# Loads of x moved into the weights' DMA queue, samples' products in another buffer, second norm's scale and shift on two engines

## The reference

```python
h = rms_norm(x, g) * (1 + sc1) + sh1
x = x + g1 * mixer(h)
h = rms_norm(x, g) * (1 + sc2) + sh2
x = x + g2 * (relu(h @ w1) ** 2 @ w2)     # 1024 -> 4096 -> 1024
```

## Time and profile before

| | us |
|---|---|
| median of 3 runs | 1322.38 (1321.24 to 1323.36) |
| profiled execution, its own time | 1323.73 |
| its span on the slowest core (core 3) | 1322.2 |
| spans of the 8 cores | 1315.9 to 1322.2 |
| TensorE busy on core 3 | 1255.1 (95%) |
| VectorE, ScalarE, GpSimd busy | 765.4, 587.5, 45.2 |

### The profile page before, as it was taken

The page is one execution under the profiler, slowest core; times in us unless marked ns, Lnnn a source line. Parts: engine busy times, 40 slices in busy tenths (PEclk is TensorE's granted clock), DMA queues, the critical chain, the costliest instruction groups (busy, mean ns, idle before and its releaser), DMA issues.

```text
span 1322.2 us, 21660 instructions; the slowest of 8 cores (1315.9 to 1322.2 us)
## 1 busy us (share of the span) xinstructions
PE 1255.1 (95%) x7558; PEld 670.3 (51%) x7558; DVE 765.4 (58%) x1478; ACT 587.5 (44%) x1088; POOL 45.2 (3%) x87
## 2 busy tenths in 40 slices
PE   3299999999999999999999999999999999999995
PEld 0156565555555555555444444554545555554543
DVE  4287856545445454577657657854545445454567
ACT  5349443433333333466443555533333333333474
POOL 0001000000000000000000000000000000000000
PEclk9999999999999999999999999999999999999998
DMA  9999936434243342502000016511303031100024
GB/s 256 193 151 171 152 53 118 92 63 96 52 78 65 64 80 49 96 1 45 20 1 1 1 32 120 105 33 32 59 7 64 1 64 29 36 1 0 1 108 164
DMA packets 23880, 91.08 MB, mean 69 GB/s; under 512 B 2768, under 2 KB 10192, under 8 KB 15696
## 3 DMA queue, kind: packets, MB, share of 16 engines
q0 software_dynamic: 9392, 67.34, 28.7%
q1 hardware_dynamic: 14384, 22.35, 5.6%
HBM read 145.43 MB, written 11.01 MB: 118 GB/s over the span
## 4 chain that ended last, share of the span: by engine, by line
PE 89%; DMA 5%; ACT 2%; DVE 2%; issue 1%; POOL 0%; SPq 0%; DVEq 0%; ACTq 0%; POOLq 0%
PE ps L977 35%; PE ps L951 34%; PE ps L1126 5%; PE ps L1097 4%; PE ps L1213 4%; PE ps L793 2%; DMA ring<-w_pack 2%; PE ps L621 2%; DMA xT_sb<-x_pack 2%; ACT hT_sb L653 1%; PE ps L583 1%; PE ps L1128 1%; DVE xT_sb L1253 1%; DMA arena<-ln_b 1%; PE ps L1179 1%
## 5 line engine op out<-in xcount | busy, mean ns | idle before, releaser
L690 DVE SCALAR_TENSOR_TENSOR xT_sb<-ps,modT,xT_sb 128x512 f32<-128x512 f32 (+3 forms) x728 | 459.0, 638 | 440.5 <-PE ps L977 393.5
L977 PE MATMUL ps<-arena,ring 128*128 128x384 bf16 (+3 forms) x2624 | 521.7, 343 | 0.1
L951 PE MATMUL ps<-hT_sb,ring 128*128 128x384 bf16 (+2 forms) x2592 | 519.7, 345 | 0.0
L957 ACT ACTIVATE arena<-ps 128x384 bf16<-128x384 f32 (+3 forms) x324 | 169.6, 527 | 497.4 <-PE ps L951 497.3
L977 PEld LDWEIGHTS ps<-arena,ring 128*128 128x128 bf16 x2624 | 253.9, 98 | 215.6 <-issue 0.6
L951 PEld LDWEIGHTS ps<-hT_sb,ring 128*128 128x128 bf16 x2592 | 251.2, 98 | 216.2
L959 ACT ACTIVATE arena<-arena 128x384 bf16<-128x384 bf16 (+3 forms) x324 | 180.6, 561 | 28.8 <-ACT arena L957 2.2
L618 ACT ACTIVATE sq<-xT_sb 128x384 bf16<-128x384 f32 (+3 forms) x216 | 105.8, 530 | 72.1 <-DVE xT_sb L690 42.1
L643 DVE TENSOR_TENSOR hT_sb<-xT_sb,rstd 128x768 bf16<-128x768 f32 (+2 forms) x80 | 75.4, 1005 | 38.9 <-ACT rstd L635 38.8
L621 PE MATMUL ps<-sq,ones 128*128 128x384 bf16 (+3 forms) x216 | 49.0, 355 | 23.0 <-ACT sq L618 20.9
L1126 PE MATMUL ps<-ring,hT_sb 128*128 128x512 bf16 x272 | 67.2, 392 | 2.6 <-ACT arena L1102 2.6
(11 more groups left out here) (91 smaller groups left out, 467.6 us busy)
## 6 DMA issues: line engine op xcount, KB each, us to landing
ring<-w_pack POOLq DMA_DIRECT2D x62, 1024.0 KB, 9.0
xT_sb<-x_pack SPq DMA_DIRECT2D x3, 1536.0 KB, 21.6
xT_sb<-x_pack SPq DMA_DIRECT2D x2, 2048.0 KB, 18.9
y_pack<-xT_sb SPq DMA_DIRECT2D x8, 512.0 KB, 2.8
y_pack<-xT_sb SPq DMA_DIRECT2D x8, 384.0 KB, 2.5
ring<-w_pool POOLq DMA_DIRECT2D x1, 1024.0 KB, 24.1
y_pack<-xT_sb SPq DMA_DIRECT2D x4, 256.0 KB, 3.1
arena<-sp_pack POOLq DMA_DIRECT2D x1, 736.0 KB, 23.1
```

The costliest lines, as they stand in the source:

```text
L690: nodes.append(S.op("dve", lambda e: e.scalar_tensor_tensor(out=xs, in0=P_(v)[:, 0:n], scalar=mcol(l, vG, dco), in1=xs, op0=ALU.mult, op1= ...
L951: mms = [(lambda e, dc=dc: e.matmul(P_(v)[:, 0:n], pv(key, 512)[:, dc, fc * 128:(fc + 1) * 128], hT.ap()[:, dc, c0:c0 + n], start=(dc == 0 ...
L957: ev = S.op("act", lambda e: e.activation(out=av, in_=P_(v)[:, 0:n], func=AF.Relu), reads=[(v.key, 0, 1)], writes=ak, cost=c_act(n), vbs=[v])
L977: mms.append((lambda e, fc=fc, av=av: e.matmul(P_(v)[:, 0:w], pv(key, 1024)[:, fc, dco * 128:(dco + 1) * 128], av, start=(fc == 0), stop=( ...
```

## The change

DMA_RATE in the planner goes from 300 to 315 KB per us. The loads of x are issued from GpSimd's queue, each planned behind the piece before it: x of g0 and g1 first, x of g2 before ada 8, x of g3 and g4 before ada 10; `GATE` is gone. The order of the pieces is changed at block 1 (w1 block 1 comes before ada 0 and 1). The due times are set anew, and `pool_z` and `pool_P` of a group stand together. The second norm's `affine` is "mix" for every group: even channel chunks on ScalarE, odd ones on VectorE. `sample_pool` writes its residual products at HH, not at H3.

```diff
@@ -24,13 +24,14 @@
 
 ENGS = ("pe", "act", "dve", "pool", "sp")
 LAT = {"pe": 0.16, "act": 0.28, "dve": 0.24, "pool": 0.3, "sp": 0.3}
-DMA_RATE = 300.0e3
+DMA_RATE = 315.0e3
 DMA_LAT = 2.2
 TABLE_BIAS = 2.5
 
 PIECES = [("ada", 0, a) for a in (2, 3)] + [("wpool", 0, 0)] + [("ada", 0, a) for a in (4, 5, 8, 9, 6, 7)] \
-    + [("w1", 0, 0), ("ada", 0, 10), ("ada", 0, 11), ("w2", 0, 0), ("ada", 0, 0), ("ada", 0, 1)]
-for _b in range(1, 8):
+    + [("w1", 0, 0), ("ada", 0, 10), ("ada", 0, 11), ("w2", 0, 0), ("w1", 0, 1), ("ada", 0, 0), ("ada", 0, 1), ("w2", 0, 1),
+       ("ada", 1, 0), ("ada", 1, 1)]
+for _b in range(2, 8):
     PIECES += [("w1", 0, _b), ("w2", 0, _b)] + [("ada", 1, a) for a in range(2 * (_b - 1), min(12, 2 * _b))]
 PIECES += [(w, 1, h) for w in ("inu", "inv", "out") for h in range(2)]
 PIECES += [(w, 1, b) for b in range(8) for w in ("w1", "w2")]
@@ -517,14 +518,20 @@
     S.op("dve", lambda e: e.memset(hT.ap()[:, :, 0:16], 0.0), writes=HK(0, 16), cost=0.3)
     xoff = [8 * t0 for (t0, n) in GR]
 
-    def load_x(g, after=()):
+    prev = [None]
+
+    def queue(node):
+        prev[0] = node
+
+    def load_x(g):
         t0, n = GR[g]
-        S.op("sp", lambda e: e.dma_start(
+        queue(S.op("pool", lambda e: e.dma_start(
             out=xT.ap()[:, :, t0:t0 + n], in_=d_xp.ap()[:, 8 * t0:8 * t0 + 8 * n].rearrange("p (c t) -> p c t", t=n)),
-            writes=XK(t0, t0 + n), stream="s_x%d" % g, cost=0.1, nbytes=4096 * n, after=after)
-
-    for g in range(3):
-        load_x(g)
+            writes=XK(t0, t0 + n), stream="s_x%d" % g, cost=0.53, nbytes=4096 * n, after=[prev[0]] if prev[0] is not None else []))
+
+    S.base = -5.0
+    load_x(0)
+    load_x(1)
     S.op("act", lambda e: e.activation(out=siluT.ap(), in_=vcol(VCT, 136).rearrange("p (a b) -> p a b", b=NSEQ), func=AF.Silu),
          reads=VR, writes=[("siluT", 0, 1)], table="silu", cost=0.4)
     S.op("dve", lambda e: e.tensor_scalar(out=vcol(VFG, 8), in0=vcol(VFG, 8), scalar1=float(np.sqrt(D)), scalar2=None, op0=ALU.mult),
@@ -537,26 +544,23 @@
 
 
     piece_vb = {}
-    prev = [None]
     S.base = -5.0
 
-    GATE = {("ada", 0, 2): 2, ("ada", 0, 8): 4}
+    XBEFORE = {("ada", 0, 8): (2,), ("ada", 0, 10): (3, 4)}
 
     def load_piece(i):
         key = PIECES[i]
         v = S.vb("ring")
         piece_vb[key] = v
-        gate = []
-        if key in GATE:
-            t0, n = GR[GATE[key]]
-            gate = XK(t0, t0 + n)
+        for g in XBEFORE.get(key, ()):
+            load_x(g)
         if key[0] == "wpool":
             n = S.op("pool", lambda e, v=v: e.dma_start(out=ring[v.slot].ap().bitcast(F32), in_=d_wp.ap()),
                      writes=[(v.key, 0, 1)], stream="w%d" % i, cost=0.53, vbs=[v], nbytes=1 << 20,
                      after=[prev[0]] if prev[0] is not None else [])
         else:
             n = S.op("pool", lambda e, v=v, i=i: e.dma_start(out=ring[v.slot].ap(), in_=d_wpk.ap()[i]),
-                     reads=gate, writes=[(v.key, 0, 1)], stream="w%d" % i, cost=0.53, vbs=[v], nbytes=1 << 21,
+                     writes=[(v.key, 0, 1)], stream="w%d" % i, cost=0.53, vbs=[v], nbytes=1 << 21,
                      after=[prev[0]] if prev[0] is not None else [])
         prev[0] = n
 
@@ -586,6 +590,7 @@
         ch = S.chain(mms, v, vbs=[pvb])
         vi, dc0 = (a * 4) // 8, (a * 4) % 8
         dst = modT.ap()[:, l, vi, dc0:dc0 + 4, :]
+        keep, S.base = S.base, (-1.0 if l == 0 else S.base)
         bb = vcol(VBA + l * 48 + a * 4, 4)
         ev = S.op("dve", lambda e: e.tensor_tensor(
             out=dst, in0=P_(v)[:, 0:128].rearrange("p (a b) -> p a b", b=32)[:, :, 0:NSEQ], in1=bcast(bb, [1, 4], [0, NSEQ]), op=ALU.add),
@@ -599,6 +604,7 @@
         if gcol is not None:
             S.op("dve", lambda e: e.tensor_tensor(out=dst, in0=dst, in1=bcast(gcol, [1, 4], [0, NSEQ]), op=ALU.mult),
                  reads=[MK(l, vi, dc0, 4)] + VR, writes=[MK(l, vi, dc0, 4)], cost=0.3)
+        S.base = keep
 
     sqi = [0]
 
@@ -797,21 +803,19 @@
             for nd in resid(0, 2, v, dco, t0, n, 0, 0):
                 S.evac(ch, nd)
 
+    S.base = -5.0
+    load_upto(("ada", 0, 10))
+    S.base = 18.0
     for a in (2, 3):
-        S.base = 34.0
         ada_piece(0, a)
-    load_upto(("ada", 0, 5))
-    S.base = -5.0
-    load_x(3, after=[prev[0]])
-    load_x(4, after=[prev[0]])
-    for g in range(5):
-        S.base = [5.0, 12.0, 20.0, 53.0, 62.0][g]
+    def zp(g):
+        S.base = [5.0, 12.0, 50.0, 86.0, 91.0][g]
         pool_z(g)
-    S.base = 14.0
-    pool_P(0)
-    S.base = 25.0
-    pool_P(1)
-    S.base = 26.0
+        S.base = [14.0, 20.0, 54.0, 90.0, 95.0][g]
+        pool_P(g)
+
+    zp(0)
+    S.base = 22.0
     wpv = piece_vb[("wpool", 0, 0)]
     Ap = bcast(modT.ap()[:, 0, 1, 0, 0:1], [NSEQ, 8])
     for q in range(2):
@@ -825,11 +829,8 @@
                 scale=Aw.ap()[:, q * 8 + k:q * 8 + k + 1]),
                 reads=[(wpv.key, 0, 1), ("Aw", q, q + 1)], writes=[(wAvb.key, q * 8 + k, q * 8 + k + 1)],
                 cost=c_act(256), vbs=[wpv, wAvb])
-    for a in (4, 5):
-        S.base = 50.0
-        ada_piece(0, a)
-    for a in (8, 9, 6, 7):
-        S.base = 70.0
+    for a, b in ((4, 32.0), (5, 36.0), (8, 57.0), (9, 63.0), (6, 70.0), (7, 77.0)):
+        S.base = b
         ada_piece(0, a)
 
     def h2_prompt(g, base):
@@ -837,16 +838,23 @@
         S.base = base
         R, RK = stats(t0, n)
         z_ops(hb(g), t0, n, R, RK)
-        affine(0, 1, hb(g), n, "act" if g < 3 else "dve")
-
-    cl = [51.0, 60.0, 70.0, 80.0, 90.0]
-    for g in range(5):
+        affine(0, 1, hb(g), n, "mix")
+
+    cl = [43.0, 51.0, 61.0, 94.0, 99.0]
+    def pm(g):
         S.base = cl[g]
         pool_mm(g)
         h2_prompt(g, cl[g] + 3.0)
-        if g + 2 < 5:
-            S.base = cl[g] + 4.0
-            pool_P(g + 2)
+
+    zp(1)
+    pm(0)
+    zp(2)
+    pm(1)
+    pm(2)
+    zp(3)
+    zp(4)
+    pm(3)
+    pm(4)
 
 
     def sample_pool():
@@ -859,7 +867,8 @@
         H4 = arB(HH, 8 * 16 * 23).rearrange("p (c b j) -> p c b j", c=8, j=23)
         S.op("pool", lambda e: e.dma_start(out=arB(HH, 2944), in_=d_spT.ap()),
              writes=[AR(HH, HH + 5888)], stream="s_sp", cost=0.53, nbytes=1507328)
-        S.base = 120.0
+        S.base = 130.0
+        load_upto(("ada", 0, 1))
         for a in (0, 1):
             ada_piece(0, a)
 
@@ -917,9 +926,9 @@
                         P_(v)[:, dq * 128:(dq + 1) * 128], Ww[:, k, oc * 128:(oc + 1) * 128], dS2[:, k, :], start=(cc == 0), stop=(cc == 1)),
                         dk + [AR(WW, WW + 4096)], 128))
             ch = S.chain(mms, v)
-            tk = [AR(H3 + hf * 2048, H3 + hf * 2048 + 2048)]
-            t4 = arF(H3 + hf * 2048, 512).rearrange("p (c b t) -> p c b t", c=4, t=8)
-            t3 = arF(H3 + hf * 2048, 512).rearrange("p (c t) -> p c t", t=128)
+            tk = [AR(HH + hf * 2048, HH + hf * 2048 + 2048)]
+            t4 = arF(HH + hf * 2048, 512).rearrange("p (c b t) -> p c b t", c=4, t=8)
+            t3 = arF(HH + hf * 2048, 512).rearrange("p (c t) -> p c t", t=128)
             ev = S.op("dve", lambda e, v=v, t4=t4, hf=hf: e.tensor_tensor(
                 out=t4, in0=P_(v).rearrange("p (c b t) -> p c b t", c=4, t=8), in1=mod_bc(0, 2, hf * 4, 4), op=ALU.mult),
                 reads=[(v.key, 0, 1), MK(0, 2, hf * 4, 4)], writes=tk, cost=c_tt(512), vbs=[v])
@@ -1258,11 +1267,11 @@
                  reads=XK(t0, t0 + n, [d, d + 1]), stream="o_y", cost=0.1, nbytes=1024 * n)
 
     load_upto(("w1", 0, 0))
-    S.base = 108.0
+    S.base = 98.0
     ada_piece(0, 10)
     ada_piece(0, 11)
     S.base = None
-    S.clk = 93.0
+    S.clk = 82.0
     mlp(0, after=lambda g: norm(1, 0, g), hooks=hooks0, first=sample_pool)
     sgu()
     mlp(1, after=final)
```

## The result

The change makes the kernel slower: a median of 1331.7 us (1330.2 to 1334.4) against 1322.21 us, ratio 1.0074 [1.0056, 1.0091]. Forecast were 1310.6 us and "faster". The profiled execution took 1330.44 us.

A forecast was written before the change was run, and what follows sets the result against it. Bound by what has landed up to 58 us, then by TensorE. 15.6 - 3.2 - 1.0 + 0.9 - 0.5 = 11.8 us off 1323.7 gave 1311.9; the runs' median lies 1.3 lower, so 1310.6 us, range 1304 to 1319.

The forecast's parts named there:

- part 3: Samples' residual products moved off H3: taking away their wait for the store is worth 0, and no wait comes in.
- Rival (b): Start: x through GpSimd's queue moves at 167 GB/s, w1 lands at 102 us; slower, 1328.0 us; chance 0.11.
- (c): GpSimd's load queue stands somewhere new for 10 to 13 us; time within 0.2% of the old; chance 0.06.
- Rival (a): ScalarE or an engine order fixed for other arrivals holds up TensorE in 85 to 115 us; 1315.6 us; chance 0.17.
- The best end of the range: No lower clock at the restart, w1 2 us earlier, no waits: 5.5 us better than forecast, 1305 us.
- Part 1: x loaded in order of need: the point where the MLP starts moves from 100.2 to 84.6 us, gaining 15.6 us.
- w1 at 84.6: The first MLP weight piece (w1 block 0) lands at 84.6 us, if the load queue never stands.
- All three are done before 84.6: Pooling of g0, g1 and g2 ends before w1 lands; g0 begins at about 41 us, g2 ends at about 75.
- Lower clock at the restart, 3.2: The MLP's first matmuls run at half rate after TensorE's scraps of 75 to 84.6 us, costing 3.2 us.
- ScalarE and orders behind 84 us, 1.0: From 84.6 us ScalarE has 27.8 of 28.3 us filled; TensorE loses 1.0 us, bounds 0 and 6.
- Part 2: Scale and shift on two engines: nothing alone beyond 0.6 us; keeps ScalarE's sum at 27.8 and not 33 us.
- Part 4: Issuing x on GpSimd: only the first load starts late, costing 0.5 us, range 0 to 4.

The follow-up runs named there:

- e2: The changed kernel with the samples' residual products back at H3; 1327.6 us, ratio 1.0039 to the kernel before.
- e1: The changed kernel with the four gating-weight multiplications (L1083) planned only after block 6 of the MLP, loads unchanged; 1317.4 us, ratio 0.9957.
- e5: The changed kernel with SyncE issuing wsp_pack before bsp_pack, engine orders otherwise the same; 1316.9 us, ratio 0.9958.
- e10: e1 with the 448 KB copy npsTa, issued beside x of g0, made to wait until about 100 us; 1313.5 us, ratio 0.9925.
- e8: e1 with the due times of g2's norm and neighbour sums set to 40 and 41 in place of 50 and 54; 1316.9 us, ratio 0.996.
- e7: e1 with the second norm's scale and shift as before the change (ScalarE for g0 to g2, VectorE for g3 and g4); 1321.9 us, ratio 1.0003.
- e6: e1 with x of g0 and g1 loaded from SyncE's queue, without a gate on the weight pieces; 1350.2 us, ratio 1.0216.

## Why the prediction was wrong

**The step that failed: part 3, "worth 0 ... no wait comes in".** It checked who reads the new address and not who takes over the old one. The wait on VectorE did go at no cost, but it had covered another: the load of `bsp_pack` over H3. That load now waits for the store, holds up `wsp_pack` in SyncE's queue, and VectorE's L1083 passes the delay on to TensorE: 16.3 us on core 5, some 15 us of the kernel's time (1331.7 against 1317.4 and 1316.9). The prediction asked who stands behind the wait on VectorE alone, and not on SyncE's queue. And "worth 0" was read from the old order: in the new one H3 costs every core some 8 us (e2), because the products run earlier.

**Sign and rivals.** Rival (b), the slower case, had another mechanism: x at 167 GB/s, w1 at 102 us. x moved at 289 GB/s (10 to 20 us) and TensorE was in w1 at 85.8. The queue did not stand either (c). Rival (a) named the right place for what is missing without the stall (85 to 115 us, orders fixed for other arrivals) and nearly its size, 1315.6 against 1316.9 and 1317.4. No rival held the stall, and the stall alone turned the sign. The best end of the range adds up to 6.2 us (3.2, 2 and 1.0), not 5.5; this changes nothing.

**Part 1: place right, size too large.** Without the stall the gain is 5.2 us (e1, e5, each against its own before) where the sum said 11.8. With the copy held back too it is 8.3 (e10). Core 4 alone is 9.8 us shorter than before (1310.2 against 1320.0), but the time follows the slowest core. Its terms:
- w1 at 84.6: right within 4 us. The eight cores began at 85.8 to 88.5, four of them behind the piece (core 5 at 87.06); core 4 was the first, at 85.8, behind VectorE's L595. The start was 2 to 3 us late, since x of g0 took until 14; e10 shows that this is the copy, which the 289 GB/s had been thought to include. With it held back the cores begin at 83.3 to 85.7, as forecast.
- "All three are done before 84.6", g2 from 62 to 75: wrong. Pooling of g0 began at 44.3, not 41, and the last matmul of g2 was at 84.0. There was no room of 9 us. x of g2 landed at 54.5 (6.19 + 48.3), near the 53.1, but ScalarE came to its squares at 61.3, behind the second norm of g0. What an earlier start of g2 would give is open, since e8 did not bring it.
- Lower clock at the restart, 3.2: did not occur on core 4 (12 matmuls in 2.38 us). TensorE had no long rest before it (0.65 us), so it was the absence of room that saved this term.
- ScalarE and orders behind 84 us, 1.0: too small. On core 4 TensorE lost 3.0 and 2.7 us in the stretches from 84 and 140 us against 1.3 and 0.4, 4.0 more. Of this 1.1 is L986 behind L706, a mild form of the stall.

**Part 2, "alone it would give nothing ... I count it there":** the credit was taken inside a sum that then came out too good. e7 prices it at 5.0 us of e1's 5.2: without it, the change would bring nothing even with the stall mended. That size is close to the 5.2 us of ScalarE's work (33 less 27.8) that the prediction counted, but this may be luck, as ScalarE is hardly the busier engine in e7.

**Part 4, 0.5 us:** the issues of x took 0.91 to 1.05 us each (two in 1.96, has 0.53 for 128 rows), at the lower end of 0.5 to 4. The rule of the Trainium skill (SBUF — State Buffer, "SBUF: two separate sides") on VectorE and the descriptors did not show: x of g3 and g4 were issued in 1.81 us with VectorE at its residuals. Whether VectorE was then in the mode that the rule speaks of no view shows.

What stays open: how much of the 15 to 23 us of `wsp_pack` is sharing with the piece, and why the store takes 18 us on one core and 24 on another. Which core is late follows from the store: if it takes over 22 us, `wsp_pack` meets the next piece. That is read from the traces of the changed kernel and of e1, not tested, and it is no sharp limit: in e8 three cores sent `wsp_pack` 0.3 to 0.6 us ahead of the piece, and it landed in 7.0 to 8.4. To hold back the pieces beside the store was not tried.

## What to carry to other kernels

When a buffer is moved to free an instruction of a wait, list everyone who touches the old bytes: a transfer may take over the wait, with a queue behind it, and work without hurry that stands early in an engine's fixed order passes its delay on. Look at the spans of all cores before a chain: here most cores stood near the forecast beside a few late ones, other ones in each execution, and the cause was a race between transfers and not the sum. And look for small copies beside the first load of a kernel: here one of 448 KB cost 3 us.

## What the runs showed of the hardware

- DMAs of two queues that are in flight together stretch each other: 1.57 MB of x took 33.4 us to land beside GpSimd's pieces (e6) and 12.4 when it stood first in their queue; 512 KB took 19.9 us beside a piece and 7.5 on a core where it went out 2.6 us ahead of it. The Trainium skill (DMA: Bandwidth & Descriptors, "Issuing engines are not separate DMA queues") says that they interleave on the same 16 engines; e6 agrees, and shows that what looks like a free choice of issuer decides the order of arrival.
- A 448 KB copy from memory to memory beside x lowered the rate between 5 and 10 us from 279 to 335 GB/s (e10) to 147 to 194 (e1), and x landed 3 us later.
- An issue of 1024 rows on GpSimd took 0.91 to 1.05 us, one of 128 rows 0.53.
- Landing times of the same DMA differ by core: `wsp_pack` took 6.1 to 19.9 us on the eight cores of one execution, the store `npsb_pack` 17.8 to 23.6.
